# Hybrid decoder step on one core: norm weights applied at an evacuation, bias copies put behind w_in

## What is computed

```python
xn = rmsnorm(x, g_attn)
c_q, c_kv, k_r, q_b, k_b, v_b, q_i, k_i, w_i = split(xn @ w_in)   # 1024 x 2024 weights
c_q  = rmsnorm(c_q, g_q);  q = c_q @ w_uq;  q_lat = q[nope] @ w_uk;  q_rope = rope(q[rope])
c_kv = rmsnorm(c_kv, g_kv); k_rope = rope(k_r)
h = x + W_out [ latent attention(q_lat, q_rope, c_kv, k_rope) | top-k attention(q_b, k_b, v_b, indexer, bias) ]
h = h + PEER(rmsnorm(h, g_ffn))      # per token 8 heads x 16 experts of 16384; rows of peer_u, peer_v gathered
y = rmsnorm(h, g_final)
```

## Time and profile before

| | |
|---|---|
| median of 3 runs | 1006.9 us |
| the profiled execution, its own time | 1008.4 us |
| its span, first to last instruction | 1006.6 us |
| mean granted TensorE clock | 0.839 |
| busy: PE, DVE, ACT, POOL | 728.6, 690.0, 401.9, 615.0 us |
| moved by DMA | 381.01 MB, mean 379 GB/s |

### The profile page before, as it was taken

How to read it: one execution, slowest core, us unless ns; L and a number is a source line. 1 busy time by engine, 2 the same in 40 slices (tenths; PEclk the granted TensorE clock), 3 DMA queues, 4 the chain that set the end, 5 groups by cost and what they waited for, 6 DMA issues and landing times.

```text
span 1006.6 us, 13868 instructions
## 1 busy us (share of the span) xinstructions
PE 728.6 (72%) x4233; PEld 366.8 (36%) x4233; DVE 690.0 (69%) x1729; ACT 401.9 (40%) x1152; POOL 615.0 (61%) x584
## 2 busy tenths in 40 slices
PE   8899997665878878866669866765586577564444
PEld 3476645221444536633213323322132244221101
DVE  2272956979687753699977698999964355667442
ACT  1163232323655771233324544653456343143322
POOL 0000476777777776476676776767776566677770
PEclk9899999788989989977767998789677788797555
DMA  9943599999999999999999999999999999999996
GB/s 344 335 160 120 204 386 410 412 413 409 411 409 408 402 412 398 403 413 381 349 361 390 406 406 408 406 405 404 409 404 407 411 415 418 412 409 409 405 410 267
DMA packets 122907, 381.01 MB, mean 379 GB/s; under 512 B 16106, under 2 KB 40762, under 8 KB 118226
## 3 DMA queue, kind: packets, MB, share of 16 engines
q0 software_dynamic: 83696, 304.81, 76.9%
q1 hardware_dynamic: 39042, 75.26, 20.1%
q10 hardware_dynamic: 96, 0.07, 0.0%
HBM read 377.90 MB, written 3.88 MB: 379 GB/s over the span
## 4 chain that ended last, share of the span: by engine, by line
DMA 28%; DVE 24%; PE 18%; POOL 15%; issue 8%; SPq 4%; ACT 3%; POOLq 0%; DVEq 0%
PE bank L471 12%; DMA rows<-in_peer_v,eid 11%; DMA rows<-in_peer_u,eid 9%; POOL rows L2023 6%; PE acc L471 5%; POOL rows L2041 5%; DVE rows L1479 5%; DMA wring<-in_w_in 3%; DMA x<-in_peer_u,eid 2%; SPq L2114 2%; DVE ql_t L1788 2%; DVE small L1787 2%; DMA z<-in_cache_kv 2%; DVE shared L1821 1%; DVE shared L1832 1%
## 5 line engine op out<-in xcount | busy, mean ns | idle before, releaser
L471 PE MATMUL acc<-rows,spread 128*64 128x512 f32 (+1 forms) x1124 | 327.9, 698 | 148.7 <-DMA rows<-in_peer_v,eid 119.8
L2023 POOL DMA_INDIRECT rows<-in_peer_v,eid x254 | 267.5, 1053 | 102.4 <-issue 70.1
L2041 POOL DMA_INDIRECT rows<-in_peer_u,eid x184 | 196.4, 1067 | 81.9 <-issue 49.4
L471 PEld LDWEIGHTS acc<-rows,spread 128*64 128x64 f32 (+1 forms) x1124 | 83.6, 154 | 318.4 <-issue 251.1
L1479 DVE CUSTOM_DVE_ANT_0 rows<-rows,xr_even 128x1024 f32<-128x1024 f32 x89 | 108.4, 1219 | 47.3 <-DMA rows<-in_peer_u,eid 46.5
L1479 DVE CUSTOM_DVE_ANT_0 rows<-rows,xr_odd 128x1024 f32<-128x1024 f32 x95 | 116.2, 1223 | 33.9 <-DMA rows<-in_peer_u,eid 33.3
L2041 POOL DMA_INDIRECT first_u<-in_peer_u,eid x37 | 40.3, 1090 | 101.0 <-DVE eid L1874 77.2
L471 PE MATMUL acc<-more_v,spread 128*64 128x512 f32 (+1 forms) x140 | 73.8, 722 | 22.3 <-DMA rows<-in_peer_v,eid 16.3
L1123 ACT ACTIVATE spread<-wide_consts,wts 128x64 f32<-128x64 f32 (+1 forms) x288 | 83.7, 338 | 4.7
L1114 ACT ACTIVATE gelus<-dots 128x2 f32<-128x2 f32 x144 | 28.6, 199 | 119.9 <-DVE dots L1479 119.4
L1116 ACT ACTIVATE wts<-gelus,gate 128x1 f32<-128x1 f32 x288 | 69.1, 287 | 4.7
(11 more groups left out here) (285 smaller groups left out, 1193.2 us busy)
## 6 DMA issues: line engine op xcount, KB each, us to landing
wring<-in_w_pq SPq DMA_DIRECT2D x12, 1024.0 KB, 8.8
z<-in_w_pq SPq DMA_DIRECT2D x5, 1024.0 KB, 8.7
wring<-in_cache_ckv SPq DMA_DIRECT2D x40, 128.0 KB
rows<-in_w_in SPq DMA_DIRECT2D x2, 2048.0 KB, 16.0
wring<-in_w_pq SPq DMA_DIRECT2D x2, 2048.0 KB, 12.5
wring<-in_w_out SPq DMA_DIRECT2D x4, 1024.0 KB, 10.3
wring<-in_cache_kv SPq DMA_DIRECT2D x32, 128.0 KB, 15.6
rows<-in_peer_v,eid POOLq DMA_INDIRECT x254, 13.6
```

Source lines behind the costliest of these rows:

```text
L471: return T.matmul(o, lhsT=l, rhs=r, start=start, stop=stop, skip_group_check=True)
L2023: nc.gpsimd.indirect_dma_start(out=v_ring[V_PLACE[n]], out_offset=None, in_=inp["peer_v"], in_offset=bass.IndirectOffsetOnAxis(ap=eid[t][: ...
L2041: nc.gpsimd.indirect_dma_start(out=u_ring[U_PLACE[n]], out_offset=None, in_=inp["peer_u"], in_offset=bass.IndirectOffsetOnAxis(ap=eid[t][: ...
```

## The change

Five edits:

1. g_q is no longer broadcast: it is loaded as a 128x3 column block (1.5 KB), the norm on DVE only scales by the root, and g_q is applied as the scale of ScalarE's evacuation of the turned c_q, in three instructions instead of one, for all three tiles.
2. The norm of c_kv and the rotary part of k_r leave `norms` for a function `latents`. For tile 0 this stands behind `x_turned(2)` and `copies(0)`, and waits for the post constants; for tiles 1 and 2 it follows `norms` directly.
3. In SP's queue the rotary table and g_kv move behind quarter 3 of w_in and w_uq; w_uq gets a semaphore of its own, for which PE waits ahead of the heads.
4. The first half of quarter 0 comes in two pieces of 512 KB, with a semaphore each.
5. POOL waits for quarter 3 of w_in before it starts the 1.5 MB bias copy `scr_d`.

```diff
-        g_q = sb("g_q_sb", [128, QL])
+        g_q = sb("g_q_sb", [128, 3])
...
             def z_product(t, c):
                 if c == 0:
-                    pe.wait_ge(w_in_half, 16)
+                    pe.wait_ge(w_in_quarter, 16)
...
                 for k in range(8):
+                    if (c, k) == (0, 2):
+                        pe.wait_ge(w_in_half, 16)
...
+            pe.wait_ge(w_uq_in, 16)
             pe.wait_ge(post_in, POST_IN)
...
             def cq_evac(t):
                 n = P[t]
                 b = ready(act, ("cq", t))
-                copy(("cq", t), cq_t[:, :, 0:n], split(b[:, 0:3 * n], 3, n))
+                if t == 0:
+                    act.wait_ge(g_q_in, 16)
+                for j in range(3):
+                    copy(("cq", t), cq_t[:, j, 0:n], b[:, j * n:(j + 1) * n], j == 2, g_q[:, j:j + 1])
...
             def norms(t):
...
-                cq_ready.send(norm(z_q, g_q[0:n, :], cqn[0:n, :], 0), t)
-                norm(z_kv, g_kv[0:n, :], ckv_nat[0:n, t, :], 1)
+                cq_ready.send(V.tensor_scalar(cqn[0:n, :], z_q, small[0:n, 0:1], None, ALU.mult), t)
+
+            def latents(t):
+
+                n, zt = P[t], zs[t]
+                norm(zt[0:n, O_CKV:O_CKV + KVL], g_kv[0:n, :], ckv_nat[0:n, t, :], 1)
                 link(V, rope(t, zt[0:n, O_KR:O_KR + 1], 1, 32, kk[0:n, IDX:IDX + 1], 32))
...
             x_turned(1)
-            dve.wait_ge(norm_in, NORM_IN)
             read_done(dve, ("z", 1, 0))
             norms(0)
             x_turned(2)
             read_done(dve, ("z", 2, 0))
             link(V, copies(0))
+            dve.wait_ge(post_in, POST_IN)
+            latents(0)
...
+            pool.wait_ge(lodge_in[3], 16)
             nc.gpsimd.dma_start(scr_d, bass.AP(scr_b.tensor, GU - 384, [[0, 128], [GU, NH], [1, WD]])).then_inc(scr_d_out, 16)
...
-            norm_consts = [(ropet[:, :, :], cst["rope"]), (g_q[:, :], bcast(inp["g_q"], QL)), (g_kv[:, :], bcast(inp["g_kv"], KVL))]
-            post_consts = [(w_uq[:, :, :], inp["w_uq"]), (uk_t[:, :, :], inp["w_uk"])]
+            post_consts = [(ropet[:, :, :], cst["rope"]), (g_kv[:, :], bcast(inp["g_kv"], KVL)), (uk_t[:, :, :], inp["w_uk"])]
...
-                    load(lodge[0][:, 0:2048], inp["w_in"][:, 0:2048], w_in_half)
+                    load(lodge[0][:, 0:1024], inp["w_in"][:, 0:1024], w_in_quarter)
+                    load(lodge[0][:, 1024:2048], inp["w_in"][:, 1024:2048], w_in_half)
                     load(lodge[0][:, 2048:4096], inp["w_in"][:, 2048:4096], lodge_in[0])
...
             lodge_columns("in", 2)
-            for o, i in norm_consts:
-                load(o, i, norm_in)
+            load(g_q[:, :], inp["g_q"], g_q_in)
             lodge_columns("in", 3)
+            load(w_uq[:, :, :], inp["w_uq"], w_uq_in)
             for o, i in post_consts:
                 load(o, i, post_in)
```

More of the change, by code:

```diff
@@ L51 @@
 WS = 1031
-FIRST_IN, HOT_IN, NORM_IN, POST_IN, CONSTS_IN = 16 * 2, 16 * 2, 16 * 3, 16 * 2, 16 * 5
+FIRST_IN, HOT_IN, POST_IN, CONSTS_IN = 16 * 2, 16 * 2, 16 * 3, 16 * 5
 NRING = 4
@@ L331, in build @@
         first_in = sem("first_consts_in")
-        w_in_half = sem("first_half_of_w_in_0_in")
+        w_in_quarter, w_in_half = sem("first_quarter_of_w_in_0_in"), sem("second_quarter_of_w_in_0_in")
+        w_uq_in = sem("w_uq_in")
         consts_in = sem("consts_in")
@@ L337, in build @@
         lodge_in = [sem(f"lodge{i}_in") for i in range(4)]
-        norm_in, out_0_in, pq_1_in = sem("norm_consts_in"), sem("first_half_of_w_out_in"), sem("second_block_of_w_pq_in")
+        g_q_in, out_0_in, pq_1_in = sem("g_q_in"), sem("first_half_of_w_out_in"), sem("second_block_of_w_pq_in")
         first_pq_in = sem("first_pq_in")
@@ L1573, in post @@
                     norms(t)
+                    latents(t)
                 link(V, rope(t, zt[0:n, O_KI:O_KI + 1], 1, 32, kk[0:n, 0:1], 32))
@@ L2060, in _ @@
             load(g_turned[:, :], inp["g_attn"], first_in)
-            norm_consts = [(ropet[:, :, :], cst["rope"]), (g_q[:, :], bcast(inp["g_q"], QL)), (g_kv[:, :], bcast(inp["g_kv"], KVL))]
-            post_consts = [(w_uq[:, :, :], inp["w_uq"]), (uk_t[:, :, :], inp["w_uk"])]
-            assert 16 * len(norm_consts) == NORM_IN and 16 * len(post_consts) == POST_IN
+            post_consts = [(ropet[:, :, :], cst["rope"]), (g_kv[:, :], bcast(inp["g_kv"], KVL)), (uk_t[:, :, :], inp["w_uk"])]
+            assert 16 * len(post_consts) == POST_IN
             consts = [(g_ffn_turned[:, :], inp["g_ffn_turned"]), (wide_c[:, :], cst["wide"]), (short_c[:, :], cst["short"]), (g_ffn[:, :], bcast(inp["g_ffn"], DM)),
@@ L2320, in laid_out @@
     a["w_pq"] = columns(a["w_pq"][0])
+    a["g_q"] = a["g_q"].reshape(3, 128).T
     a["w_uk"] = a["w_uk"][0].reshape(KVL, HR, 128).transpose(2, 1, 0)
```

## The result

The changed kernel takes 1014.75 us (median of 6 runs, 1014.12 to 1016.85). Six runs of the kernel before, three of them new, give 1007.59. The ratio is 1.0075, 95% interval 1.0064 to 1.0086: slower by 0.75%, where the forecast was 1000.7. The profiled execution took 1014.34 us.

What follows compares the result with a forecast made beforehand. Gathers filling the DMA engines were taken to bound the kernel, so only their earlier start helps: 6.7 - 0.4 - 0.1 = 6.2 us, against the median of 1006.9 giving 1000.7 us; range 998.9 to 1004.2.

Steps and rivals of the forecast that it cites:

- the last of the sum: First gather, issued at 112.85 us, comes 6.2 us earlier, and the DMA-full stretch behind it moves with it.
- Norm weights: Start, VectorE: c_q norm waits for no load, ready at about 30.1 us; TensorE's wait of 2.73 us goes.
- last quarter: Start, w_in: lands by 31.6 us instead of 38.96; TensorE's 1.30 us wait goes, last product takes 6.70.
- The reason for the late loads: Start: 265 GB/s from 20 to 34 us against 409 before, full engines shared with GpSimd's 1.5 MB bias copy.
- Split of the first quarter: TensorE's w_in product at 10.54 us is not waiting for w_in, so an earlier first piece is worth 0.
- (a) Post constants: Start, tile 0: rotary table, g_kv, w_uk and w_uq in by 36.3 us, before TensorE's 41.69; cost 0.
- (b) Stores: First attention block's exponentials may wait for tile 0's stores, seen landed at 59.99 us; cost 0.4, between 0 and 0.7.
- (c) Bias table: Loaded behind the bias copy, in at 60.5 us, before VectorE's first use at 65.1; cost 0.
- (d) Three evacuations: c_q on ScalarE: at most 1.0 us more per tile; counted as 0.1 for tiles 1 and 2 together.
- Given back among the gathers: Earlier gathers meet other weight loads or buffer order, last slices end as before: gain 0 to 2 us; 11%.
- the slower rival: Lengthened copies bring the bias table in at 76.1 us, first attention block ends 4.7 later: 1011.6 us; 4%.

Runs made afterwards that it cites:

- a_w256: Changed kernel with 480 unused bytes ahead of the weight ring, which again starts 256 past a multiple of 512 bytes: 1000.65 us.
- a_pad384: Changed kernel with g_q's tile allocated 384 columns wide (three used), so every later tile keeps its old address: 1004.31 us, ratio 0.9966.
- a512_nowait: Changed kernel with every large tile at a multiple of 512 bytes and without GpSimd's wait ahead of the bias copy: 991.29 us.
- b_all512: Kernel before, with gaps that put every large tile at a multiple of 512 bytes, start order unchanged: 995.4 us.

## Why the prediction was wrong

**The step that failed** is the last of the sum: "so 112.85 moves by 6.2, and with it the full stretch behind". The first half was right in kind and too small: 7.37 us. The second half took the rate of the full stretch as given; its reason stands in the prediction's second paragraph, that such a stage "ends earlier only if it starts earlier". The forecast gave 85% to a faster kernel, and the measured one is slower, because that rate fell from 407 to 393 GB/s between 550 and 800 us. That it can move with the kernel's tiles was nowhere costed: the g_q edit was priced as a smaller load, a shorter evacuation and one operand less, and its first line, a tile of 3 columns, as nothing. That line takes 9 us between 550 and 850 us in the profiled executions (from -5.3 to +3.9 in the table above) and costs 10 to 14 us in the medians (1014.75 against 1004.31 and 1000.65 to 1001.21 with the ring back at its boundary). With the ring where it had been, a_w256 took 1000.65, beside the forecast's 1000.7. That so close a match is partly luck shows in a_pad384: there every tile is where it had been, and it took 1004.31, 0.1 above the forecast's range.

The other parts, in the prediction's order:

- *Norm weights, last quarter:* both waits went and the product took 6.72 us, forecast 6.70; the last quarter was in by 28.56, forecast 31.6. The heads began 7.27 us earlier, forecast 6.71. The rest is quarter 2, taken up 0.27 us earlier, and the c_q turn, which runs on from the transposes without a gap, 0.3 us.
- *The reason for the late loads* was half right. The copy did take half of the engines' time (53.1%) beside the small packets. In a512_nowait it runs beside the loads as well, takes 32.6%, and TensorE does not wait: moving the small loads is what counts, and GpSimd's wait bought nothing that these runs can tell.
- *Split of the first quarter, 0:* not undone by itself. TensorE begins the product at 10.41 instead of 10.54, with no idle time ahead of it in either.
- *(a) Post constants, 0:* right, VectorE ran on from 35.22 to 35.25 without a wait.
- *(b) Stores, 0.4:* it was 0. The stores landed before 57.83, 2.1 us earlier than the 59.99 of before, and the exponentials waited longer for VectorE. The rule of the Trainium skill weighed there (page "DMA: Bandwidth & Descriptors", section "Issuing engines are not separate DMA queues") would have left them at 59.99. That transfers interleave is what the traces show; that the order of the issues changes nothing does not follow, since a queue of small packets moves less in the same time.
- *(c) Bias table, 0:* right. Its load was issued at 45.17 and took 10.9 us (in by 56.1, forecast 60.5), and the mask addition ran at 64.00 without a wait (forecast 65.1).
- *(d) Three evacuations:* 0.89 us instead of 0.49, beside the last product; the 0.1 for tiles 1 and 2 was not read apart.
- *The rivals:* none named the layout. "Given back among the gathers" had the place but not the mechanism, and held the loss to the whole gain; the slower rival (4%) has the right sign for the wrong reason, since the bias table was in time.

The Trainium skill, page "DMA: Bandwidth & Descriptors", section "How a descriptor splits into AXI transactions", has the rule that was not weighed: a descriptor that starts at a multiple of 256 bytes goes in pieces of 256, and one that does not starts with a piece at the boundary below. Estimated from that rule of the Trainium skill, off the boundary 8 KB would be 33 pieces instead of 32 (3.1%), 4 KB 17 instead of 16 (6.3%) and 1 KB 5 instead of 4 (25%). The traces agree in the boundary (256 is enough, 128 is not). In the size they come near for 8 KB alone: 316 against 309 ns, 2.3%; rows off the boundary cost 4 KB packets 2.0% (162.7 against 159.5 ns), and the 1 KB pages took 47.6 against 46.3 ns, 2.8%. The Trainium skill tells it of reads; here the side off the boundary is the one written. So the boundary is shown by the runs, and this reason for it is not. That section of the Trainium skill does not say why the gathers' own packets slow down when other tiles are off: those of the changed kernel go to the same places as those of a_w256 and take 166.8 against 160.9 ns. That packets for the ring hold up packets for the rows on a path they share would fit; it was not tried by itself.

## What to carry to other kernels

A tile that becomes smaller moves every tile allocated behind it: compare the addresses of before and after as part of the change, and hold them still (a padded tile) when an edit elsewhere is to be measured. Where transfers are what bounds a stage, put the tiles that they write at multiples of 256 bytes; here three gaps of 192 columns in all (b_all512) were worth 10 to 11 us (995.4 and 997.5 against 1006.6 and 1007.5), twice what the reordered start brought. Loads in small packets ahead of a load that is needed soon can cost more than a large copy on another queue: here moving them won the start, and holding the copy back won nothing on top.

## What was not expected of the hardware

- A full stretch moved 393 or 407 to 408 GB/s at the same DMA share of 1.04, by 32 bytes in the place of tiles in SBUF; with the rows aligned too, 412.
- Packets of 8 KB took 309 ns (median, 150 to 300 us) for a tile at a multiple of 256 bytes and 314 to 316 off it; from 550 to 800 us gather packets of 4 KB took 159.4 on average with everything aligned, 161 with only the ring aligned and 166 to 167 with neither.
- The same copy of 1.5 MB left SP's queue 2.01 or 3.58 MB in the same 14 us, with small packets in that queue or with packets of 9 to 16 KB; its own packets of 4596 bytes took 333 or 206 ns.
